# Rounding remainders of weight tiles on VectorE inside the attention and recurrence stages, and a norm's sum of squares by one matmul a half

## The reference

```python
for i in range(2):                                     # first network
    h = modulate(rms_norm(x, ln_ffn1[i]), sh1, sc1)
    x = x + 0.5 * g1 * swiglu(h, ffn1_wg[i], ffn1_wu[i], ffn1_wd[i])   # hidden width 2816
    h = modulate(rms_norm(x, ln_mix[i]), sh2, sc2)
    mix = diff_attention(h, ...) if i == 0 else spatial_gating(h, ...)
    x = x + g2 * mix
    h = modulate(rms_norm(x, ln_ffn2[i]), sh3, sc3)
    x = x + 0.5 * g3 * swiglu(h, ffn2_wg[i], ffn2_wu[i], ffn2_wd[i])
    x = rms_norm(x, ln_out[i])
# second network
h = rmsnorm(x, norm_mix)
q, f, i, g = split(h @ w_in, 4)                        # w_in 1024 x 4096
log_f = logaddexp(log(lb), log1p(-lb) + log_sigmoid(f)); k = (1 - lb) * sigmoid(-f)
# per head of 128: S_t = diag(f_t) S_{t-1} + k_t v_t^T ; o_t = S_t^T q_t
x = x + (rmsnorm_per_head(o) * out_norm * silu(g)) @ w_out
x = x + squared_relu_mlp(rmsnorm(x, norm_mlp), w1, w2)
out = rmsnorm(x, norm_final)
```

## Time and profile before

| | before |
|---|---|
| median of 3 runs | 2725.0 us (2724.41 to 2728.86) |
| the profiled execution | 2722.24 us, its span 2720.2 us |
| mean granted PE clock in it | 0.983 |
| PE busy | 2651.3 us (97%), 13119 matmuls |
| DVE, ACT, POOL busy | 1024.0, 887.2, 1079.3 us |
| moved from HBM | 306.44 MB, 114 GB/s over the span |

### The profile page before, as it was taken

How to read it: one execution, slowest core, us unless ns; L and a number is a source line. 1 busy time by engine, 2 the same in 40 slices (tenths; PEclk the granted TensorE clock), 3 DMA queues, 4 the chain that set the end, 5 groups by cost and what they waited for, 6 DMA issues and landing times.

```text
span 2720.2 us, 31206 instructions
## 1 busy us (share of the span) xinstructions
PE 2651.3 (97%) x13119; PEld 2222.6 (82%) x13119; DVE 1024.0 (38%) x1439; ACT 887.2 (33%) x1354; POOL 1079.3 (40%) x436
## 2 busy tenths in 40 slices
PE   7999999999999999999999999999999999999998
PEld 6888888776788888888888988888887778888887
DVE  2634244445432324634344354111164454512213
ACT  1322224555422223322224343222343222423322
POOL 0444443222344544444443435444433222344442
PEclk7999999999999999999999999999999999999999
DMA  5655343211333333445443224332231111222231
GB/s 193 227 183 180 133 156 106 77 63 47 109 124 124 124 132 128 172 146 182 137 169 112 95 93 140 99 99 97 79 96 63 47 52 58 77 94 96 99 100 62
DMA packets 252002, 310.58 MB, mean 114 GB/s; under 512 B 7197, under 2 KB 231214, under 8 KB 251863
## 3 DMA queue, kind: packets, MB, share of 16 engines
q1 hardware_dynamic: 248874, 304.93, 33.1%
q10 hardware_dynamic: 2988, 3.66, 0.4%
HBM read 306.44 MB, written 4.74 MB: 114 GB/s over the span
## 4 chain that ended last, share of the span: by engine, by line
PE 95%; DVE 3%; ACT 1%; issue 1%; DMA 0%; SPq 0%; POOL 0%; DVEq 0%; ACTq 0%
PE bank L1641 27%; PE bank L1642 26%; PE bank L1643 26%; PE bank L1586 2%; PE bank L1675 1%; PE bank L1676 1%; PE bank L1677 1%; PE bank L1790 1%; PE bank L1506 1%; PE bank L1526 1%; PE bank L1613 1%; DVE scr L1110 1%; PE bank L1766 1%; PE bank L1495 1%; DVE scr L1109 0%
## 5 line engine op out<-in xcount | busy, mean ns | idle before, releaser
L703 POOL TENSOR_TENSOR w_lo_t<-w_raw,w_hi_t 128x1024 fp32r<-128x1024 f32 (+1 forms) x432 | 1079.1, 2518 | 1609.8 <-ACT w_hi_t L856 1609.5
L1641 PE MATMUL bank<-h_hi,w_hi_t 128*128 128x512 f32 (+1 forms) x2160 | 846.4, 392 | 6.3 <-DVE h_lo L1226 2.9
L1642 PE MATMUL bank<-h_lo,w_hi_t 128*128 128x512 f32 (+1 forms) x2160 | 822.1, 381 | 0.0
L1643 PE MATMUL bank<-h_hi,w_lo_t 128*128 128x512 f32 (+1 forms) x2160 | 821.7, 380 | 0.0
L856 ACT CAST w_hi_t<-w_raw 128x1024 fp32r<-128x1024 f32 (+1 forms) x432 | 424.8, 1032 | 702.3 <-PE bank L1643 666.6
L1641 PE MATMUL bank<-act_hi,w_hi_t 128*128 128x512 f32 (+1 forms) x1264 | 474.7, 376 | 10.8 <-POOL w_lo_t L703 5.6
L1641 PEld LDWEIGHTS bank<-h_hi,w_hi_t 128*128 128x128 f32 x2160 | 410.3, 190 | 90.0 <-issue 13.4
L1643 PEld LDWEIGHTS bank<-h_hi,w_lo_t 128*128 128x128 f32 x2160 | 409.3, 189 | 77.7
L1642 PE MATMUL bank<-act_lo,w_hi_t 128*128 128x512 f32 (+1 forms) x1264 | 469.9, 372 | 0.0
L1642 PEld LDWEIGHTS bank<-h_lo,w_hi_t 128*128 128x128 f32 x2160 | 410.4, 190 | 72.8 <-issue 3.1
L1643 PE MATMUL bank<-act_hi,w_lo_t 128*128 128x512 f32 (+1 forms) x1264 | 469.8, 372 | 0.0
(11 more groups left out here) (233 smaller groups left out, 2075.7 us busy)
## 6 DMA issues: line engine op xcount, KB each, us to landing
scr<-in_ada_w SPq DMA_DIRECT2D x128, 512.0 KB, 6.7
w_raw<-in_ffn_wg SPq DMA_DIRECT2D x44, 1024.0 KB, 5.2
w_raw<-in_ffn_wu SPq DMA_DIRECT2D x44, 1024.0 KB, 5.2
w_raw<-in_ffn_wd SPq DMA_DIRECT2D x32, 1024.0 KB, 5.2
w_raw<-in_mlp_w SPq DMA_DIRECT2D x32, 1024.0 KB, 5.3
w_raw<-in_hgrn_w_in SPq DMA_DIRECT2D x16, 1024.0 KB, 5.4
w_raw<-in_ffn_wd SPq DMA_DIRECT2D x16, 768.0 KB, 4.3
w_raw<-in_attn_w_qkv SPq DMA_DIRECT2D x12, 1024.0 KB, 5.1
```

What stands on the lines that cost most here:

```text
L703: nc.gpsimd.tensor_tensor(w_lo_t[:, t % 2, k], w_raw[:, t % 2, k], w_hi_t[:, t % 2, k].bitcast(F32), ALU.subtract).then_inc(w_lo, 1)
L1641: pe.matmul(dst, w_h, m_h, start=first, stop=False)
L1642: pe.matmul(dst, w_h, m_l, start=False, stop=False)
L1643: return pe.matmul(dst, w_l, m_h, start=False, stop=last)
```

## The change

Two things are changed.

Of the remainders of the tiles that the attention and recurrence stages read, those of tiles 2 to 11 of the attention's 12 and of tiles 2 to 15 of the recurrence's 16 are taken by DVE instead of POOL. Each is cut in quarters of two blocks (128x512 elements, `rest_quarter`), and each quarter is a step of the written sequence, placed 2, 3, 3 and 4 fills after the tile's "conv". They have a semaphore of their own, `w_rest`; PE's `w_half` and SP's `weight` wait for it where the tile is one of these, and the counts of `w_lo` leave these tiles out.

In every norm DVE adds the squares of blocks 6 and 7 to `ssq` too, half by half (`ssq_half`), so that `sum_squares` has one matmul of its own sum in each half instead of three, and the one of 512 columns for a folded pre-norm is one instead of three; the pre-norm's own three in each half stay. For half 0 of all norms but the first the squares of blocks 6 and 7 are written to PSUM banks 0 and 1 instead of `sq`. DVE's adds for half 0 stand between `x_half` of block 6, and of block 7, and for half 1 among the first blocks of the norm. The sum of half 1 stands ahead of block 3 instead of block 2.

```diff
--- before.py
+++ after.py
@@ -186,6 +186,8 @@
 
 
 AT_WO_EARLY = 6
+AT_RESTS = 10
+AT_REST_AT = (2, 3, 3, 4)
 NAT_BANKS = ((0, 1, 3, 6), (4, 5, 2, 7))
 
 
@@ -204,6 +206,10 @@
 
     def flush_convs():
         seq.extend(convs)
+        for _, i in convs:
+            if i < AT_RESTS:
+                for q, k in enumerate(AT_REST_AT):
+                    after(k, ("rest", i, q))
         del convs[:]
 
     def unit_done(u):
...
@@ -291,6 +300,10 @@
 
     def flush_convs():
         seq.extend(convs)
+        for _, i in convs:
+            if i < HG_RESTS:
+                for q, k in enumerate(HG_REST_AT):
+                    after(k, ("rest", i, q))
         del convs[:]
 
     def unit_done(u):
...
@@ -552,12 +567,33 @@
             w = ins[name][layer]
             return w[row:row + kb * P, :].rearrange("(k p) n -> p k n", p=P)
 
+        def last_square(n, kb, half):
+
+            if n and half == 0:
+                return ps[kb - 6][:, 0:HS]
+            return sq[:, kb % 2, half * HS:half * HS + HS]
+
         n_tiles = T
         tile_kb = [KB] * T
         for op in ops:
             if op.kind == "down":
                 tile_kb[op.t0:op.t0 + 4] = [op.kb] * 4
 
+        rests = [t for op in ops if op.kind in ("attn", "hgrn")
+                 for t in range(op.t0 + 2, op.t0 + 2 + (AT_RESTS if op.kind == "attn" else HG_RESTS))]
+
+        def on_dve(t):
+
+            return t in rests
+
+        def rest_tiles(t):
+
+            return sum(r < t for r in rests)
+
+        def pool_tiles(t):
+
+            return t - rest_tiles(t)
+
         def half_rows(t, hf):
 
             return slice(4, tile_kb[t]) if hf else slice(0, 4)
@@ -569,7 +605,10 @@
             def weight(slot, t, src, kb=KB, skip_wait=False):
 
                 if not skip_wait:
-                    sp.wait_ge(w_lo, 2 * (t - 1))
+                    if on_dve(t - 2):
+                        sp.wait_ge(w_rest, 4 * rest_tiles(t - 1))
+                    else:
+                        sp.wait_ge(w_lo, 2 * pool_tiles(t - 1))
                 sp.dma_start(w_raw[:, slot, 0:kb, :], src).then_inc(raw_in[slot], 16)
 
             def ada_step(s):
@@ -697,7 +736,7 @@
         def _(pool):
 
             for t in range(n_tiles):
-                for hf in range(2):
+                for hf in range(0 if on_dve(t) else 2):
                     k = half_rows(t, hf)
                     pool.wait_ge(w_hi, 2 * t + hf + 1)
                     nc.gpsimd.tensor_tensor(w_lo_t[:, t % 2, k], w_raw[:, t % 2, k], w_hi_t[:, t % 2, k].bitcast(F32),
...
@@ -880,8 +919,8 @@
             def square_half(n, kb, half, x_count, pre=None, npre=0):
                 cols = slice(half * HS, half * HS + HS)
                 act.wait_ge(x_upd, x_count)
-                act.wait_ge(ssq_done, 5 * n + kb - 2)
-                act.activation(sq[:, kb % 2, cols], blk(x, kb)[:, cols], ACT.Square).then_inc(sq_done, 1)
+                act.wait_ge(ssq_done, 9 * n + kb - 2)
+                act.activation(last_square(n, kb, half), blk(x, kb)[:, cols], ACT.Square).then_inc(sq_done, 1)
                 if pre is not None:
                     act.wait_ge(pre_ssq_done, 5 * npre + kb - 2)
                     act.activation(pre_sq[:, kb % 2, cols], blk(x, kb)[:, cols], ACT.Square,
@@ -1036,6 +1075,13 @@
         def v_scratch(small_t):
             return small_t[:, 5:6]
 
+        def rest_quarter(dve, t, q):
+
+            rows = slice(2 * q, 2 * q + 2)
+            dve.wait_ge(w_hi, 2 * t + q // 2 + 1)
+            dve.tensor_tensor(w_lo_t[:, t % 2, rows], w_raw[:, t % 2, rows], w_hi_t[:, t % 2, rows].bitcast(F32),
+                              ALU.subtract).then_inc(w_rest, 1)
+
         def attn_dve(dve, op, link):
             def combine(n):
 
@@ -1048,7 +1094,9 @@
 
             dve.wait_ge(bias_d, 16 * (1 + 2 * HEADS))
             for step in attn_sequence():
-                if step[0] == "qk":
+                if step[0] == "rest":
+                    rest_quarter(dve, op.t0 + step[1] + 2, step[2])
+                elif step[0] == "qk":
                     u = step[1]
                     j, k = attn_unit(u)
                     n = 4 * j + k
...
@@ -1190,6 +1240,14 @@
                     else:
                         dve.wait_ge(pre_ssq_done, 5 * npre + kb - 1)
                         dve.tensor_tensor(pre_ssq, pre_ssq, pre_sq[:, kb % 2, :], ALU.add).then_inc(pre_ssq_done, 1)
+
+            def ssq_half(n, kb, half):
+
+                k = 2 * half + kb - 6
+                cols = slice(half * HS, half * HS + HS)
+                dve.wait_ge(sq_done, 10 * n + 7 + k)
+                dve.wait_ge(ssq_done, 9 * n + 5 + k)
+                dve.tensor_tensor(ssq[:, cols], last_square(n, kb, half), ssq[:, cols], ALU.add).then_inc(ssq_done, 1)
 
             def x_half(op, kb, half):
 
@@ -1282,6 +1340,9 @@
                 dve.tensor_copy(blk(x, kb), ps[kb][:]).then_inc(x_upd, 1)
                 if 1 <= kb <= 6:
                     ssq_add(0, kb - 1)
+            for half in range(2):
+                for kb in (6, 7):
+                    ssq_half(0, kb, half)
             dve.wait_ge(init_a, 1)
             for kb in range(KB):
                 if kb % 2 == 0:
@@ -1330,6 +1391,9 @@
                         h_low(op, *order[k])
                         if k == 1 and late:
                             x_half(late, 7, 1)
+                            ssq_half(op.n0, 6, 1)
+                        if k == 2 and late:
+                            ssq_half(op.n0, 7, 1)
                     if op.pre:
                         dve.wait_ge(pre_root, pres + 1)
                         pres += 1
@@ -1347,6 +1411,8 @@
                                .then_inc(fin_x, 1)
                             if half == 0 and kb == 2:
                                 x_half(op.down, 7, 1)
+                            if half == 0 and kb in (3, 4):
+                                ssq_half(op.n0, kb + 3, 1)
                     for tb in range(TB):
                         dve.wait_ge(fin_t, 2 * tb + 2)
                         dve.tensor_copy(fin_nat[:, tb, S:2 * S], ps[(2 * tb + 1) % 4][:]).then_inc(fin_c, 1)
@@ -1392,8 +1458,9 @@
                             ssq_add(op.n0, nb - 1, op.pre, pres)
                     if op.last:
                         ssq_add(op.n0, 5, op.pre, pres)
-                        x_half(op, 6, 0)
-                        x_half(op, 7, 0)
+                        for kb in (6, 7):
+                            x_half(op, kb, 0)
+                            ssq_half(op.n0, kb, 0)
                 elif op.kind == "attn":
                     attn_dve(dve, op, link)
                 elif op.kind == "sgu":
@@ -1644,7 +1711,10 @@
 
             def w_half(t, hf):
 
-                pe.wait_ge(w_lo, 2 * t + hf + 1)
+                if on_dve(t):
+                    pe.wait_ge(w_rest, 4 * rest_tiles(t) + 2 * hf + 2)
+                else:
+                    pe.wait_ge(w_lo, 2 * pool_tiles(t) + hf + 1)
 
             def unit(dst, slot, b, m_hi, m_lo, kbs=KB, wait_k=None, tile=None, groups=(), op=None):
 
@@ -1696,12 +1766,9 @@
             def sum_squares(n, half, pre, npre):
 
                 dst, cols = ps[6 + half][:, 0:HS], slice(half * HS, half * HS + HS)
-                pe.wait_ge(ssq_done, 5 * (n + 1))
-                pe.wait_ge(sq_done, 10 * n + 8 + 2 * half)
+                pe.wait_ge(ssq_done, 9 * n + 7 + 2 * half)
                 own = ones if pre is None else eps_ones
-                pe.matmul(dst, own[:], ssq[:, cols], start=True, stop=False)
-                pe.matmul(dst, own[:], sq[:, 0, cols], start=False, stop=False)
-                mm = pe.matmul(dst, own[:], sq[:, 1, cols], start=False, stop=pre is None)
+                mm = pe.matmul(dst, own[:], ssq[:, cols], start=True, stop=pre is None)
                 if pre is not None:
                     pe.wait_ge(pre_ssq_done, 5 * (npre + 1))
                     pe.wait_ge(pre_sq_done, 10 * npre + 8 + 2 * half)
@@ -1710,9 +1777,7 @@
                     mm = pe.matmul(dst, ones[:], pre_sq[:, 1, cols], start=False, stop=True)
                 mm.then_inc(ssum_mm, 1)
                 if pre is not None and half:
-                    pe.matmul(ps[3][:], ones[:], ssq[:], start=True, stop=False)
-                    pe.matmul(ps[3][:], ones[:], sq[:, 0, :], start=False, stop=False)
-                    pe.matmul(ps[3][:], ones[:], sq[:, 1, :], start=False, stop=True).then_inc(pre_mm, 1)
+                    pe.matmul(ps[3][:], ones[:], ssq[:], start=True, stop=True).then_inc(pre_mm, 1)
 
             def half_unit(dst, slot, b, half, kbs, kb0=0, kb1=None):
 
@@ -1728,7 +1793,7 @@
                 for half in range(2):
                     cols = slice(half * HS, half * HS + HS)
                     for kb in range(KB):
-                        if half == 0 and kb == 2 and norm.down:
+                        if half == 0 and kb == 3 and norm.down:
```

(10 more changed lines are left out.)

4 lines of the change are left out of this document (2 added, 2 removed).

## The result

| | before | after |
|---|---|---|
| median | 2726.93 us (2724.41 to 2729.02, 4 runs) | 2701.15 us (2697.95 to 2702.32, 4 runs) |
| ratio, 95% interval | | 0.9904 [0.9887, 0.9921] |
| profiled execution, its span | 2722.24, 2720.2 us | 2701.66, 2699.8 us |

The change makes the kernel 25.8 us faster by the medians (forecast 2704.6, measured 2701.15) and 20.6 us by the two profiled executions, where the sum of the prediction was 20.4.

The account below looks back on a forecast made before the run. PE, busy 97% of the span, was taken to bound the kernel. From 2722.24 us, -20.9 (remainders) and +0.5 (sums) gave 2701.8 profiled, 2704.6 as median; own range 2698 to 2711, 2696 to 2715 for 8 in 10.

Parts of the forecast that it names:

- collisions in the recurrence up to tile 16: Five places where PE waits for DVE multiplies held by POOL's subtractions; removing waits and low clock gains 22.8 us.
- quarters in the recurrence: 56 DVE subtractions of 0.685 us make PE's level 3 0.6 us later in pairs 1 to 3: 1.9 us cost.
- attention: 40 quarters on DVE in the attention stage fit into idle time: 0 us, bounds -0.5 to +2.
- five plain norms: Norms without folded pre-norm: two DVE adds of 0.40 us less 0.2 saved, +0.6 each, +3.0 us.
- pre-norm ahead of layer 1: Norm before the first layer-1 stage: adds go mostly into DVE's wait for half 1's root, +0.2 us (-0.2 to +0.6).
- pre-norm ahead of the recurrence: Norm before the recurrence goes by PE; fewer sum matmuls save until DVE is later: -2.4 us (0 to -2.8).
- prologue: Kernel start: four fewer sum matmuls save 3.4 us, losing the upper-clock stretch behind them costs 3.4: 0 us.
- the rival that it stays low: Recurrence: small waits remain and keep the lower clock, so 9 us aren't gained: 2714 us, chance 0.14.
- The rival that the change doesn't do what it says: Recurrence: POOL doesn't cause the 2.75 us multiplies, waits stay, quarters and adds are paid: 2727 us, chance 0.04.
- one of the signs of being wrong: DVE waiting for ACT's w_hi ahead of a level would show the prediction wrong; no size given.
- The DVE-queue rival: Recurrence and attention: quarters waiting for ACT's rounding hold the next level multiply; 2748 us, or 2726 for half; chance 0.08.
- The rival that it stays: Prologue keeps its upper-clock stretch despite fewer sum matmuls: 3.4 us more gained, 2701 us, chance 0.12.

Follow-up runs that it names:

- fills: Kernel before, with POOL writing zero fills instead of subtracting for tiles 2 to 15 of the recurrence, their remainders left out: 2699.91 us, ratio 0.9905.
- part one: Changed kernel with the sums of squares as before, so only the attention's and recurrence's remainders move to DVE: 2699.25 us, ratio 0.9902 to before.
- the doubled quarters: Remainders on DVE, sums of squares as before, each quarter of the recurrence's 14 tiles taken twice: 2712.28 us, ratio 0.9947 to before.
- part two alone: Changed kernel with all remainders back on POOL, so only the one-matmul sums of squares differ from before: 2729.02 us, ratio 1.0007.

## Why the prediction was right, point by point

| term | forecast | measured |
|---|---|---|
| collisions in the recurrence up to tile 16 | -22.8 | -25.0 (fills) |
| quarters in the recurrence | +1.9 | +0.9 (to 2300, part one less fills) |
| attention | 0 | 0.0 |
| five plain norms | +3.0 | -0.3 |
| pre-norm ahead of layer 1 | +0.2 | +2.4 (after), +3.3, +3.1 |
| pre-norm ahead of the recurrence | -2.4 | -0.6 (after), +1.0, +0.9 |
| last norm | -0.3 | -0.6 |
| prologue | 0 | -0.1 |
| behind the attention (not in the sum) | | +2.8, the execution's |

**Collisions.** Right in place and mechanism. By the fills, the two places of 6.2 us measured 6.3 each, that of 4.5 was 4.7, those of 2.1 and 3.8 were 2.15 and 3.75. Missing was L1099, of 128x1024 elements. It lay beside POOL in all four pairs, 2.25 us long in the first and 1.48 in the others, and takes 1.23 beside the fills: PE gets 1.0 us back at the first pair and 0.25 at each of the other three. These 1.8 us are what the places, 23.2 us in all, lack of 25.0. (The clock's share of the forecast is 9.6 us by its own terms, not "about 9"; by the fills it was 9.9.) The clock came back with the waits, so the rival that it stays low is out: 1.00 from 2030 to 2250. The rival that the change doesn't do what it says fell by the fills.

**Quarters.** The duration was exact. The wait at level 3 is 0.42 us, not 0.62, and against the fills kernel PE is 0.5 us later there in each of the pairs 1 to 3. No product of PE waited for `w_rest`. SP's loads did, 24 times, as they had waited for POOL, but nothing of PE was held by it. Something near one of the signs of being wrong showed: at three places (2079.46, 2148.42 and 2217.40 in after) DVE stood 9.0 us and then began four quarters as soon as ACT's w_hi was there. It cost nothing: these places lie between two pairs of heads, with no level right behind them, and PE's only wait between 2060 and 2100 is one of 0.6 us. The DVE-queue rival did not happen, but it was nearer than it looked: the doubled quarters show that 2.1 us more of DVE at one level in each of three pairs cost 14.0 us.

**Plain norms.** Mis-sized by 0.6 each. In half 0, where I had written 0.2 to 0.3 us of gain, there are 0.6. DVE's add starts when ACT's square ends, is 0.42 us long, and PE's sum starts at 442.38, where it had started at 442.26. Before, PE went 0.30 us behind ACT's end; now it goes 0.06 behind DVE's. With after 0.06 us ahead at that point, the add costs 0.2 us, not 0.5.

```profile
441.90 0.42 DVE L1250 TENSOR_TENSOR ssq<-bank,ssq 128x256 f32<-128x256 f32 x1 [0.46 <-ACT bank L923]
```

```profile
442.38 0.70 PE L1771 MATMUL bank<-ssq,ones 128*128 128x256 f32 x2
```

Above are DVE's and PE's timelines of after. In half 1 the two adds cost about 0.55, not 0.8. So a plain norm gains at half 0 what it gives back at half 1.

**Pre-norms.** Here the step that failed is the saving of 2.6 us "until DVE is the later". PE was the later engine only while it ran the sums, and both norms end in a wait of PE for a chain that does not start with the sums. Ahead of the recurrence PE reached that wait early and stood 2.65 us for ACT instead of 0.91. At 2000 us the 2.4 us of the forecast had been gained in full; the longer wait gave 1.7 of them back. PE's timelines, after and then before:

```profile
2013.50 0.47 PE L1708 MATMUL bank<-h_hi,w_hi_t 128*128 128x512 f32 x1 [2.65 <-ACT scr L836]
```

```profile
2009.20 0.47 PE L1641 MATMUL bank<-h_hi,w_hi_t 128*128 128x512 f32 x1 [0.91 <-ACT scr L797]
```

The chain of waits of before showed 2 x 0.43 + 2 x 0.86 us of PE there, and I took it as PE's to gain without following what comes next, 11 us on. Ahead of layer 1 the step "DVE waits for half 1's root there and then is the start of a chain" was right, and the term was still mis-sized: it left out the longer load and the clock behind the longer wait, 1.0 and 1.5 us.

**Prologue.** As forecast: the sums are 3.4 us shorter, the upper stretch goes, and after is 0.1 us ahead at 58.6. The rival that it stays is out. The two stretches of after, in the columns of the earlier trace rows:

```profile
30.60:48.70 18.10, 18.10 (x75) 15.85 (x76) 7.96 (x16) 3.73 (x7) 1.78 (x1) 0.50 0.69 223
48.70:58.30 9.60, 9.60 (x46) 9.60 (x47) 0.00 (x0) 0.00 (x0) 2.89 (x2) 0.50 0.00 0
```

Part one alone keeps the upper stretch and part two alone loses it, and at 58.6 they stand at -0.30 and -0.35. Three other traces, one of them without part two, stand at -1.2 to -1.4 there, so differences under 1.4 us in the prologue belong to the execution.

**The sum.** Against the trace of after, the gain of the recurrence was put 3.0 us too low (23.9 measured) and the cost of the plain norms 3.3 too high, the cost of the pre-norms 4.0 too low, and 2.8 us of clock belong to the execution. The errors nearly cancel, -20.6 against -20.4. The median came out 3.5 us under the forecast, because I had put it 2.8 us over the profiled execution and it lay 0.5 us under it. The gain by the medians is larger than by the profiles, 25.8 for 20.6, as before's profiled execution lay 4.7 us under its median.

## What to carry to other kernels

Where a VectorE multiply with both inputs in SBUF takes four times its length, look at what GpSimd reads at that moment, and price the place as wait plus the clock behind it; moving GpSimd's work onto a VectorE that has idle slots, in pieces that fit them, takes it away whole. Before taking work off TensorE, follow it to its next wait: if what it waits for doesn't start with that work, the wait gets longer by as much, and in some executions a longer wait costs clock on top. One profiled execution can hold 3 us of clock that the next does not, so a term of that size needs several traces of like kernels side by side.

## What the runs showed of the hardware

This subtraction on VectorE is not held when one operand is in PSUM: in before, 17 of `act_lo<-bank,act_hi` lay beside POOL's remainders at 0.68 to 0.69 us, while `act_lo<-scr,act_hi`, both in SBUF, took 2.83 beside them and 0.69 elsewhere.

What a wait of TensorE costs in clock isn't told by its length alone. From 1000 us on, the waits of over 0.9 us in PE's timelines of the 14 traces, and how many of them had the lower clock 3 us behind them:

| wait, us | lower clock behind |
|---|---|
| 0.9 to 1.3 | 0 of 25 |
| 1.55 to 1.6 | 5 of 12 |
| 1.97 | 4 of 4 |
| 2.1 to 2.75 | 22 of 32 |
| 2.8 to 2.9 | 17 of 19 |
| 4.7 to 5.1 | 3 of 3 |

The waits of 1.97 us and those five of 1.6 stand in the last norm, where PE has little else to do. Short waits aren't safe everywhere either: one of 1.17 us at the attention's end, at 655, among short matmuls, had it in 9 of 11 traces. One and the same wait, 2.10 us ahead of the output projection's third tile, had it in some traces and not in others. The Trainium skill (TensorE: Matmul & The Clock Gate, Part 1) has the lower level as the default and lets activity release it; that the lower level shows here behind waits, and at the ends of stages with little work for PE, agrees with it.
